# Two transformer blocks on one Trainium2 core: the eleven lanes of steps merged in another order

## The chip, the cores and the metric

The kernel runs on one core of one Trainium2 chip. Its time is the time of one execution on the device, in microseconds (us); lower is better. The profile shows one execution as the hardware profiler recorded it. Engines: PE is TensorE (matmuls), PEld its loads of weights, DVE VectorE, ACT ScalarE, POOL GpSimd, SP SyncE (it issues the loads from HBM).

## What is computed

Two blocks follow each other on 256 rows of width 1024, all in float32, each block with two layers. A layer of the first block runs a sparse attention and a gated delta rule side by side and mixes them:

```python
h = rms_norm(x, norm_gain[layer]);  proj = h @ w_in[layer]          # split into 12 parts
y_a = dsa_attention(q_a, k_a, v_a, q_i, k_i, w_i) * silu(z_a)       # attention over the top keys
qkv_b = silu(causal_depthwise_conv(qkv_b, conv_w[layer]))
o_b = chunked_gated_delta_rule(l2_normalize(q_b), l2_normalize(k_b), v_b, beta, g)
y_b = rms_norm(o_b, gdn_norm_gain[layer]) * silu(z_b)
x = x + (gates[0] * y_a + gates[1] * y_b) @ w_out[layer]
```

The result, normalised once more, is the memory `mem`; the second block starts from it with four branches per layer (latent attention, stick-breaking attention, forgetting attention, attention over the memory):

```python
h = x @ w_in                                   # split into 9 parts
mk, mv = split(mem @ w_mem_kv)
merged = sum(sigmoid(merge_r @ w_merge_up)[n] * ((y[n] * silu(gate_z[n])) @ w_branch[n]) for n in range(4))
x = layer_norm(alpha * x + merged @ w_out)
```

## The kernel before

**The products.** Each float32 operand is written as a higher and a lower part, and a product is three matmuls: high by high, high by low, low by high. The weights come in units: one unit is two rows of 128 by 512 of a weight matrix (the names in the code are a matrix and a place in it, as mkv.6, o1.2, h3.4, br21). For one unit SP loads `raw` (five buffers), ACT copies it to the higher part `w_hi` (L1347), POOL subtracts to get the lower part `w_lo` in two halves (L866, L868), and PE multiplies (`mm`, L907; matmuls in L926, L934, L941). `w_hi` and `w_lo` have three slots, so a split waits until PE has used the unit three before it. The order of the units is fixed by their lane.

**The other steps.** Between the units PE makes small products of the attentions and of the delta rule, and transposes (L962), in two halves of PSUM called `chain`, which steps take in turn: a step first waits until the step two before it has been emptied by ACT or DVE (`take`, L951). Steps that the text names: `hT`, `xT` transpose the normalised rows at the start of a layer; `norm_a`, `norm`, `norm_c` are the norm's steps on DVE and ACT (L1668 to L1674 are the four tiny operations of its square root, L1753 the scaling); `mix_b`, `mix`, `mT` mix the two paths (L2207, L2223) and transpose the result for w_out; `onorm` is the norm of the delta rule's output; `stat_1_0` its key's transposes after the convolution (`tap`, `conv`); `gT` transposes the merged branches of the second block; `lat_a`, `lat`, `lat_c` normalise its latents (L2256 is the scaling), `ckT` transposes them; `sbz` are the scores of the stick-breaking attention, emptied by L2269 and L2272; `ln_a`, `ln_s`, `ln` are the layer norm at the layer's end; `gmul` the gate's product on DVE; `drain` empties a bulk product; `gz`, `mu`, `br`, `o`, `h` are weight matrices.

**The order of the work.** `lanes()` (L299) writes the steps into eleven lanes, each with a fixed inner order: s splits, m bulk products, d and v their drains on ACT and DVE, c convolution, w gates, a and b chains, x mix, y merge, e layer norm. `ORDER` (L319) is a string with one letter per step, and `plan()` (L335) takes the next step of the lane that the letter names. Every engine then walks the one list and runs those steps for which it has a handler:

```python
def plan():
    steps = {lane: iter(x) for lane, x in lanes().items()}
    return [next(steps[lane]) for lane in ORDER]
...
            for step in PLAN:
                if step[2] in steps:
...
                    steps[step[2]](*step[3:])
```

Engines wait for each other by semaphores; the value that a wait wants is the step's place among those of its name in the list. So the order sets which step stands behind which on each engine, and nothing else.

Of the kernel before, what the change touches and what calls it, by code (L numbers as in the profile page):

```python
# [298 lines left out]
def lanes():  # L299
# [17 lines left out]


ORDER = (  # L319
    "aaaaasammssvamsmssaamaaasaacsccasscccssammcmmsmaacssmmaacssccsmmmamaaasasmdabsmaaabssmmcsmaammassdbm"  # L320
    "adbmssaaammsssammsbadamsabaamamsaaaamssacmasccmaamasbsbbmacccscmammssmsccsaacbcmmbssmambbsaaasssammb"
    "bdsaaaamsssdmmmmaassdwbbssmmmsamcbmmamssssbbdbbmmaaambabxxsasbmaabbbsddmxssbaamswwamaaamaassmamsdwaa"
    "mwbasxsxmmsdmsaxbmwxsaxxxbmbbmxaxvsvsssmssmmmammsmaammsdsaaammsssssvammmmaaaascasscmmsccasscmcassccm"
    "msmaammcmsacsmcasmsassdaaaammasassmmaambbsmambacmaaamdassmssbdbssmaamabammaaamssaaadmsscamacsmssssaa"
    "mmamccacccmssbbscbcmmcamssacammbbsssmabbsmaaamdssaaaammssdsammadmmaabbscbbbmaswmmssdsbbbaassmsssmaaw"
    "maabmmbambsbxmxxbmssdbbbmmsssdamawammaasaadswwmbamasxxbsamaamssbaxdbbwxsxxmmmxxxsssssvsmmsvasadmmmmm"
    "mmsaaaasassaassmmdsssssdssbsdsbbmmmmmmsmmmmammmmsssaassdaasmmbbsaadbbsmmmbsaaasmmbddabbmbbmssaaamvba"
    "bmbsssddmmbbadmmsssybbmbssbmaambdsymsbamdsyyavbymbysydvvmmyssdmvssvvvvdmsvvvdmmmmssdymmmmmmvvvssssss"
    "yvvsmmmmmmmvmmmvsseeessvvvvaeeessmmaaammmbmmmmmmssdmssssssssdmmmmmadsasmsbaaammmbbbaassdasssdbbmbmma"
    "asaamsbmbsddbmbbmaaabmsssvbbmbasmmsabbdmbddsssasmabbssmymmambayddssmbsmbdsssydvyysmsdbsyyvvmmydmmmmv"  # L330
    "svsmdvvvvmsvvyssssmmvvvmmyvvmvvmssemmmmmsseemmvvvveemmme"
)


# [2132 lines left out]
```

How the kernel before makes its waits and increments, by code:

```python
                def load(u):  # L802
                    name, w, k0, nk, _, _ = UNITS[p.sec][u]
                    old = raw_before(p, u)
                    if old:
                        sp.wait_ge(*o.after("gpsimd", old[0], old[1], "split", old[2]))
                    src = dview(w["src"], p.l)
                    if w["src"] == "w_branch":
                        k0 += 2 * int(w["lhs"][2])
# [15 lines left out]
                def load_memory(g, r):  # L825
                    if (p.l, g, r) == (0, 1, 0):
                        sp.wait_ge(*p.after("tensor", "vT", 1))
                        sp.dma_start(mem_raw, t["mem_2"].rearrange("a (r p) d -> p (a r) d", p=P)).then_inc(mem_in, 16)
# [1 line left out]
                def next_gain():  # L830
                    sp.wait_ge(*p.after("vector", "norm_c", 1))
                    if p.l == 0:
                        load_more()
                    load_gain(t["gains"][p.l + 1:p.l + 2, :])
# [1 line left out]
                def ln_rows():  # L836
                    sp.wait_ge(*o.after("vector", "mid", 0, "norm_c", 1))
                    if p.l:
                        sp.wait_ge(*o.after("vector", "two", p.l - 1, "ln", 1))
                    for i, dst in enumerate((gain, gain2)):
                        sp.dma_start(dst[:, :], t["ln_rows"][2 * p.l + i:2 * p.l + i + 1, :].broadcast_to([P, D])).then_inc(
                            ln_in, 16)
# [130 lines left out]
                def memT(r):  # L974
                    if r == 0:
                        pe.wait_ge(mem_in, 16)
                    c = take("memT", r)
```

## Time and profile before

| | us |
|---|---|
| median of three runs (lowest to highest) | 1060.01 (1059.55 to 1061.75) |
| span of the profiled execution | 1056.6 |
| PE busy | 1025.6 (97%) |
| POOL busy | 712.2 (67%) |
| DVE busy | 599.0 (57%) |
| ACT busy | 577.4 (55%) |

The profiled execution has its span alone, from the first instruction to the last; the runs were timed from outside and lie 3.4 us above it. Busy time says which engine carries the program; what can still be moved is read from the waits of that engine, and from what else ran beside the instruction that was waited for.

### The profile page before, as it was taken

How to read it: one execution, taken by the hardware profiler on the slowest of the kernel's cores; microseconds unless marked ns; L12 is line 12 of the kernel's file. 1: busy time of each engine (PE TensorE's matmuls, PEld its weight loads, DVE VectorE, ACT ScalarE, POOL GpSimd, SP SyncE). 2: the span in 40 equal slices, each digit the busy share in tenths (PEclk: the TensorE clock that was granted, in tenths of full speed). 3: DMA queues.
4: the chain of work that ended last, by engine and by line, in shares of the span. 5: the costliest groups of instructions: out<-in, count | busy, mean ns of one | idle time of the engine just before them, and what ended most of it. 6: DMA issues, size and time to landing. Idle time of an engine off the chain costs nothing.

```text
span 1056.6 us, 18561 instructions
## 1 busy us (share of the span) xinstructions
PE 1025.6 (97%) x7112; PEld 886.4 (84%) x7112; DVE 599.0 (57%) x1181; ACT 577.4 (55%) x968; POOL 712.2 (67%) x550
## 2 busy tenths in 40 slices
PE   8999999999999999999999998999999989999986
PEld 8988998888877988899888887788888768888875
DVE  4774366786565557246584563517446560646564
ACT  4754347656644574336656744445576534567652
POOL 4786537872648787556766645897366978744794
PEclk9999999999999999999999999999999999999999
DMA  8664434653425555435444332665233546423451
GB/s 294 192 179 122 139 101 131 173 156 107 134 100 153 180 165 157 140 84 157 141 139 141 115 125 87 209 191 158 81 113 120 186 140 216 133 91 108 140 183 57
DMA packets 80584, 151.59 MB, mean 143 GB/s; under 512 B 6448, under 2 KB 12400, under 8 KB 80496
## 3 DMA queue, kind: packets, MB, share of 16 engines
q1 hardware_dynamic: 80496, 150.41, 46.9%
q8 instruction: 57, 0.93, 0.4%
q14 instruction: 31, 0.25, 0.1%
HBM read 149.34 MB, written 1.05 MB: 142 GB/s over the span
## 4 chain that ended last, share of the span: by engine, by line
PE 88%; DVE 4%; ACT 3%; POOL 3%; issue 2%; DMA 0%; POOLq 0%; SPq 0%; DVEq 0%; ACTq 0%
PE bulk L941 53%; PE bulk L926 12%; PE chain L962 5%; PE chain L970 4%; PE chain L1039 4%; PE chain L1307 1%; PE bulk L934 1%; PE chain L1288 1%; ACT arena L1347 1%; PE chain L1163 1%; PE chain L1179 1%; POOL w_lo L868 1%; DVE arena L1846 1%; PE chain L1030 1%; POOL w_lo L866 1%
## 5 line engine op out<-in xcount | busy, mean ns | idle before, releaser
L866 POOL TENSOR_TENSOR w_lo<-raw,w_hi 128x512 fp32r<-128x512 f32 (+3 forms) x259 | 340.7, 1316 | 292.4 <-ACT w_hi L1347 291.8
L868 POOL TENSOR_TENSOR w_lo<-raw,w_hi 128x512 fp32r<-128x512 f32 (+3 forms) x277 | 375.6, 1357 | 31.8 <-ACT w_hi L1347 31.8
L1347 ACT ACTIVATE w_hi<-raw 128x1024 fp32r<-128x1024 f32 (+4 forms) x277 | 277.3, 1019 | 210.1 <-PE bulk L941 163.4
L941 PE MATMUL bulk<-w_hi,hT_hi 128*128 128x512 f32 (+1 forms) x756 | 306.0, 405 | 0.8 <-ACT arena L1347 0.5
L941 PE MATMUL bulk<-w_hi,hT_lo 128*128 128x512 f32 (+1 forms) x756 | 294.4, 389 | 0.0
L941 PE MATMUL bulk<-w_lo,hT_hi 128*128 128x512 f32 (+1 forms) x756 | 204.2, 389 | 1.9 <-POOL w_lo L868 1.9
L941 PEld LDWEIGHTS bulk<-w_hi,hT_hi 128*128 128x128 f32 x756 | 142.4, 188 | 33.5 <-issue 1.9
L941 PEld LDWEIGHTS bulk<-w_lo,hT_hi 128*128 128x128 f32 x756 | 141.7, 188 | 32.7 <-POOL w_lo L868 3.4
L941 PEld LDWEIGHTS bulk<-w_hi,hT_lo 128*128 128x128 f32 x756 | 142.5, 188 | 26.8 <-issue 1.0
L926 PE MATMUL bulk<-hT_hi,w_hi 128*128 128x256 f32 x384 | 96.3, 289 | 0.0
L926 PE MATMUL bulk<-hT_lo,w_hi 128*128 128x256 f32 x384 | 94.0, 282 | 0.0
L962 PE MATMUL chain<-cst,arena 128*128 128x128 f32 (+1 forms) x544 | 73.4, 276 | 7.8 <-DVE arena L2223 3.5
L962 PEld LDWEIGHTS chain<-cst,arena 128*128 128x128 f32 (+1 forms) x544 | 62.7, 142 | 15.1 <-issue 9.3
L926 PEld LDWEIGHTS bulk<-hT_hi,w_hi 128*128 128x128 f32 x384 | 73.4, 191 | 0.9 <-ACT w_hi L1347 0.7
L1347 ACT ACTIVATE arena<-chain 128x512 f32<-128x512 f32 (+4 forms) x64 | 45.5, 727 | 52.0 <-PE chain L962 23.6
L926 PEld LDWEIGHTS bulk<-hT_lo,w_hi 128*128 128x128 f32 x384 | 73.5, 191 | 0.0
L1846 DVE SCALAR_TENSOR_TENSOR arena<-bulk,par,arena 128x253 f32<-128x253 f32 (+2 forms) x144 | 59.4, 475 | 21.0 <-ACT arena L1347 19.0
L1342 ACT ACT_TABLE_LOAD x44 | 56.5, 1283 | 26.5 <-PE bulk L941 14.3
L1347 ACT ACTIVATE arena<-bulk 128x1024 f32<-128x1024 f32 (+2 forms) x50 | 50.1, 1006 | 17.3 <-PE bulk L941 17.2
L926 PE MATMUL bulk<-hT_hi,w_lo 128*128 128x256 f32 x384 | 53.9, 283 | 0.0
L1347 ACT ACTIVATE arena<-arena,tiny 128x256 f32<-128x256 f32 (+1 forms) x80 | 36.2, 454 | 27.0 <-DVE tiny L2345 19.4
L926 PEld LDWEIGHTS bulk<-hT_hi,w_lo 128*128 128x128 f32 x384 | 49.5, 192 | 0.0
(262 smaller groups left out, 1393.4 us busy)
## 6 DMA issues: line engine op xcount, KB each, us to landing
raw<-in_w_in_dram SPq DMA_DIRECT2D x194, 512.0 KB, 3.6
raw<-in_w_out_dram SPq DMA_DIRECT2D x32, 512.0 KB, 3.7
raw<-in_w_branch_dram SPq DMA_DIRECT2D x16, 512.0 KB, 3.7
raw<-in_w_mem_kv_dram SPq DMA_DIRECT2D x8, 512.0 KB, 3.4
raw<-in_w_merge_up_dram SPq DMA_DIRECT2D x16, 256.0 KB, 2.9
raw<-in_w_in_dram SPq DMA_DIRECT2D x8, 420.0 KB, 3.4
gain<-in_ln_rows_dram SPq DMA_DIRECT2D x4, 512.0 KB, 5.3
gain<-in_gains_dram SPq DMA_DIRECT2D x3, 512.0 KB, 6.1
```

What stands on the lines that cost most here:

```text
L866: pool.tensor_tensor(lo_of(p, u)[:, 0:at], raw_of(p, u)[:, 0:at], hi_of(p, u)[:, 0:at].bitcast(F32), ALU.subtract).then_inc(first_part, 1)
L868: pool.tensor_tensor(lo_of(p, u)[:, at:n], raw_of(p, u)[:, at:n], hi_of(p, u)[:, at:n].bitcast(F32), ALU.subtract).then_inc(p.done("split" ...
L926: m = pe.matmul(dst, part[:, k, j * P:(j + 1) * P], b[:, kk, :], start=(not low and kk == 0 and i == 0 and j % 2 == 0), stop=(low and kk = ...
L934: m = pe.matmul(pair[0:n, 0:S], part[:, k, :], b[:, kk, :], start=(not low and kk == 0 and i == 0), stop=(low and kk == tot - 1))
L941: m = pe.matmul(dst, a, part[:, k, :], start=(first and not low and k == 0 and i == 0), stop=(last and low and k == nk - 1))
L962: m = pe.transpose(c[0:n, i * P:i * P + v.shape[0]], v, ident[0:v.shape[0], 0:v.shape[0]])
L970: m = pe.matmul(c[at, col + j * HALF:col + (j + 1) * HALF], a, b, start=(j == 0), stop=(j == R * 4 - 1), skip_group_check=True)
L1030: pe.matmul(c[:, j * P:(j + 1) * P], spread(4 * r + j, 8), rows_T[0:8, :], start=(j == 0), stop=(j == 3), skip_group_check=True)
L1039: m = pe.matmul(c[:, j * P:(j + 1) * P], a, b, start=(j == 0), stop=(j == 3), skip_group_check=True)
L1342: act.preload_act_table_set(sets[func])
L1347: return act.activation(dst, src, func, **more)
L1846: ins = STT(cv[:, j, back:S], b[:, j * S:(j + 1) * S - back], par1[:, p.l, c:c + 1], cv[:, j, back:S], ALU.mult, ALU.add)
```

## The change

`ORDER` is another string, of the same letters, each as often as before. Nothing else differs: lanes, handlers, buffers and waits are the same code. Of its twelve lines one:

```diff
 ORDER = (
-    "aaaaasammssvamsmssaamaaasaacsccasscccssammcmmsmaacssmmaacssccsmmmamaaasasmdabsmaaabssmmcsmaammassdbm"
+    "aaaaasavssmmaamsamsmasasasaacmmmccscsmacccassaamsmcmsssmaacmcmscmamassadssabammsaaacammmasmsmmbmdssa"
...
```

At the change of layer in the first block, on ACT, from the last splits of layer 0 on (`hT_hi<-chain` empties the transposes hT, `w_hi<-raw` are splits, the last three wide ones before hT being mkv.2, mkv.4 and mkv.6, `mkv<-bulk` empties that product). Before:

```order
L1347 ACTIVATE w_hi<-raw 128x1024 [waits mm_tensor,raw_in2]
L1347 ACTIVATE arena,tiny<-xs 128x1024 [waits drain_v_vector,x_loaded]
L1347 ACTIVATE w_hi<-raw 128x1024 [waits mm_tensor,raw_in3]
L1347 ACTIVATE tiny<-tiny 128x2 [waits norm_a_vector]
L1347 ACTIVATE tiny<-tiny 128x2 [waits scalar_step]
L1347 ACTIVATE w_hi<-raw 128x1024 [waits mm_tensor,raw_in4]
L1347 ACTIVATE mkv<-bulk 128x1024 [waits mm_tensor]
L1347 ACTIVATE w_hi<-raw 128x704 [waits mm_tensor,raw_in0]
L1347 ACTIVATE hT_hi<-chain 128x1024 [waits rows_turned_tensor] x2
```

And now:

```order
L1347 ACTIVATE w_hi<-raw 128x1024 [waits mm_tensor,raw_in2]
L1347 ACTIVATE w_hi<-raw 128x1024 [waits mm_tensor,raw_in3]
L1347 ACTIVATE arena,tiny<-xs 128x1024 [waits drain_v_vector,x_loaded]
L1347 ACTIVATE tiny<-tiny 128x2 [waits norm_a_vector]
L1347 ACTIVATE tiny<-tiny 128x2 [waits scalar_step]
L1347 ACTIVATE hT_hi<-chain 128x1024 [waits rows_turned_tensor]
L1347 ACTIVATE w_hi<-raw 128x1024 [waits mm_tensor,raw_in4]
L1347 ACTIVATE hT_hi<-chain 128x1024 [waits rows_turned_tensor]
L1347 ACTIVATE w_hi<-raw 128x704 [waits mm_tensor,raw_in0]
L1347 ACTIVATE w_hi<-raw 128x1024 [waits mm_tensor,raw_in1]
L1347 ACTIVATE mkv<-bulk 128x1024 [waits mm_tensor]
```

The split of mkv.6 (raw_in4) and the emptying of its product have moved behind the emptying of the transposes.

At the end of layer 1 of the first block, on ACT, from the emptying of the last gate product on (`gain<-bulk`; `arena,tiny<-arena` are the sums of squares of `onorm_a`, the table load and the tiny operations are `onorm`, raw_in1 is unit o1.2, the last row empties mT_1). Before:

```order
L1347 ACTIVATE hT_hi<-chain 128x1024 [waits rows_turned_tensor,mm_tensor]
L1347 ACTIVATE gain<-bulk 128x1024 [waits gmul_vector,mm_tensor]
L1347 ACTIVATE arena,tiny<-arena 128x128 [waits o_vector]
L1347 ACTIVATE arena,tiny<-arena 128x128 [waits scalar_step] x7
L1347 ACTIVATE w_hi<-raw 128x1024 [waits mm_tensor,raw_in1]
L1342 ACT_TABLE_LOAD [waits onorm_a_vector]
L1347 ACTIVATE tiny<-tiny 128x2x4
L1347 ACTIVATE tiny<-tiny 128x2x4 [waits scalar_step]
```

And now:

```order
L1347 ACTIVATE gain<-bulk 128x1024 [waits gmul_vector,mm_tensor]
L1347 ACTIVATE hT_hi<-chain 128x1024 [waits rows_turned_tensor,mm_tensor]
L1347 ACTIVATE arena,tiny<-arena 128x128 [waits o_vector]
L1347 ACTIVATE arena,tiny<-arena 128x128 [waits scalar_step] x7
L1342 ACT_TABLE_LOAD [waits onorm_a_vector]
L1347 ACTIVATE tiny<-tiny 128x2x4
L1347 ACTIVATE tiny<-tiny 128x2x4 [waits scalar_step]
L1347 ACTIVATE w_hi<-raw 128x1024 [waits mm_tensor,raw_in1]
```

The gate product is emptied ahead of the transposes mT_0, and the split of o1.2 has moved behind the table load and the norm's two operations.

In layer 1 of the second block, on DVE, at the latents (L1668 to L2256 are `lat_c`, the pairs L2269 and L2272 empty `sbz`). Before:

```order
L2269 SCALAR_TENSOR_TENSOR arena<-chain,cst 128x1024
L2272 SCALAR_TENSOR_TENSOR arena<-arena 128x1024
L2269 SCALAR_TENSOR_TENSOR arena<-chain,cst 128x512
L2272 SCALAR_TENSOR_TENSOR arena<-arena 128x512
L1668 TENSOR_TENSOR tiny<-tiny 128x4
L1670 TENSOR_TENSOR tiny<-tiny 128x4
L1672 TENSOR_SCALAR tiny<-tiny 128x4
L1674 TENSOR_TENSOR tiny<-tiny 128x4
L2256 SCALAR_TENSOR_TENSOR arena<-arena,tiny,par 128x384 x2
L2256 SCALAR_TENSOR_TENSOR arena<-arena,tiny,par 128x256 x2
```

And now:

```order
L1668 TENSOR_TENSOR tiny<-tiny 128x4
L1670 TENSOR_TENSOR tiny<-tiny 128x4
L1672 TENSOR_SCALAR tiny<-tiny 128x4
L1674 TENSOR_TENSOR tiny<-tiny 128x4
L2256 SCALAR_TENSOR_TENSOR arena<-arena,tiny,par 128x384 x2
L2256 SCALAR_TENSOR_TENSOR arena<-arena,tiny,par 128x256 x2
L2269 SCALAR_TENSOR_TENSOR arena<-chain,cst 128x1024
L2272 SCALAR_TENSOR_TENSOR arena<-arena 128x1024
L2269 SCALAR_TENSOR_TENSOR arena<-chain,cst 128x512
L2272 SCALAR_TENSOR_TENSOR arena<-arena 128x512
```

`lat_c` has moved ahead of the emptying of both `sbz`.

## Rows read from the trace of the kernel before

**Rows 1.** The page, busy time of the engines, and the chain by engine.

```profile
PE 1025.6 (97%) x7112; PEld 886.4 (84%) x7112; DVE 599.0 (57%) x1181; ACT 577.4 (55%) x968; POOL 712.2 (67%) x550
...
PE 88%; DVE 4%; ACT 3%; POOL 3%; issue 2%; DMA 0%; POOLq 0%; SPq 0%; DVEq 0%; ACTq 0%
```

**Rows 2.** What PE waited for, whole span; us in total, times, longest us.

```profile
PE chain L962 <- DVE arena L2223: 3.5, 2, 2.9
...
PE chain L962 <- DVE arena L1828: 2.7, 1, 2.7
...
PE bulk L934 <- DVE hT_lo L1759: 1.4, 1, 1.4
```

**Rows 3.** PE's timeline; start, us, engine, line, operation, tiles, count, [idle before <-releaser].

```profile
635.47 0.39 PE L941 MATMUL bulk<-w_hi,hT_hi 128*128 128x512 f32 x1
...
638.19 0.39 PE L941 MATMUL bulk<-w_hi,hT_hi 128*128 128x512 f32 x1
...
643.92 1.94 PE L962 MATMUL chain<-cst,arena 128*128 128x128 f32 x8 [2.85 <-DVE arena L2223]
...
645.51 0.78 PE L941 MATMUL bulk<-w_hi,hT_hi 128*128 128x512 f32 x1
...
649.08 0.39 PE L941 MATMUL bulk<-w_hi,hT_hi 128*128 128x512 f32 x1
```

**Rows 4.** DVE's timeline, layer norm at the change of layer in block one.

```profile
334.38 1.21 DVE L1670 TENSOR_TENSOR tiny<-tiny 128x2 f32<-128x2 f32 x1
...
335.62 1.22 DVE L1672 TENSOR_SCALAR tiny<-tiny 128x2 f32<-128x2 f32 x1
...
336.88 1.20 DVE L1674 TENSOR_TENSOR tiny<-tiny 128x2 f32<-128x2 f32 x1
```

**Rows 5.** POOL's timeline, the same stretch.

```profile
334.29 1.28 POOL L868 TENSOR_TENSOR w_lo<-raw,w_hi 128x512 fp32r<-128x512 f32 x1
...
336.78 1.28 POOL L868 TENSOR_TENSOR w_lo<-raw,w_hi 128x512 fp32r<-128x512 f32 x1
```

**Rows 6.** POOL's and DVE's timeline, the layer norm ahead of block two.

```profile
668.81 1.29 POOL L868 TENSOR_TENSOR w_lo<-raw,w_hi 128x512 fp32r<-128x512 f32 x1
...
670.16 0.16 DVE L1674 TENSOR_TENSOR tiny<-tiny 128x2 f32<-128x2 f32 x1
```

**Rows 7.** ACT's timeline, the end of layer 1 of block one.

```profile
635.73 1.06 ACT L1347 ACTIVATE w_hi<-raw 128x1024 fp32r<-128x1024 f32 x1 [0.96 <-PE bulk L941]
...
636.81 1.28 ACT L1342 ACT_TABLE_LOAD   x1
```

**Rows 8.** PE's timeline, two single waits, at stat_1_0 and at gz1.0.

```profile
380.81 1.06 PE L962 MATMUL chain<-cst,arena 128*128 128x128 f32 x8 [0.69 <-ACT arena L1347]
...
773.36 0.50 PE L941 MATMUL bulk<-w_hi,hT_hi 128*128 128x512 f32 x1 [0.53 <-ACT arena L1347]
```

**Rows 9.** DVE's timeline, the mix at the ends of layers 0 and 1.

```profile
288.52 2.19 DVE L2223 TENSOR_TENSOR arena<-arena 128x1024 f32<-128x1024 f32 x1
...
640.23 2.19 DVE L2207 SCALAR_TENSOR_TENSOR arena<-arena,tiny 128x128 f32<-128x128 f32 x8
...
642.55 1.22 DVE L2223 TENSOR_TENSOR arena<-arena 128x1024 f32<-128x1024 f32 x1
```

**Rows 10.** DVE's timeline, L2256 in layers 0 and 1 of block two.

```profile
715.19 4.86 DVE L2256 SCALAR_TENSOR_TENSOR arena<-arena,tiny,par 128x384 f32<-128x384 f32 x4
...
911.32 1.94 DVE L2256 SCALAR_TENSOR_TENSOR arena<-arena,tiny,par 128x384 f32<-128x384 f32 x4
```

**Rows 11.** Stretches: busy us of PE, PEld, DVE, ACT, POOL; PEclk, DMA share, GB/s.

```profile
645.00:646.00 1.00, 1.00 (x6) 0.99 (x5) 0.00 (x0) 0.05 (x1) 0.00 (x0) 0.50 0.00 0
```

**Rows 12.** ACT's timeline, change of layer in block two.

```profile
863.71 1.99 ACT L1347 ACTIVATE w_hi<-raw 128x1024 fp32r<-128x1024 f32 x2
```

**Rows 13.** DVE's timeline, eviction of sbz_0 in layer 1 of block two.

```profile
907.41 1.69 DVE L2272 SCALAR_TENSOR_TENSOR arena<-arena 128x1024 f32<-128x1024 f32 x1
```

**Rows 14.** POOL's timeline, start of its last unbroken run.

```profile
1010.39 1.37 POOL L866 TENSOR_TENSOR w_lo<-raw,w_hi 128x512 fp32r<-128x512 f32 x1 [0.86 <-ACT w_hi L1347]
```

More of the change, by code:

```diff
@@ L319 @@
 ORDER = (
-    "aaaaasammssvamsmssaamaaasaacsccasscccssammcmmsmaacssmmaacssccsmmmamaaasasmdabsmaaabssmmcsmaammassdbm"
[L321 to L329, printed above, removed]
@@ L330 @@
-    "asaamsbmbsddbmbbmaaabmsssvbbmbasmmsabbdmbddsssasmabbssmymmambayddssmbsmbdsssydvyysmsdbsyyvvmmydmmmmv"
-    "svsmdvvvvmsvvyssssmmvvvmmyvvmvvmssemmmmmsseemmvvvveemmme"
+    "aaaaasavssmmaamsamsmasasasaacmmmccscsmacccassaamsmcmsssmaacmcmscmamassadssabammsaaacammmasmsmmbmdssa"
+    "dsabbsambssamsaaasmamaabsadamamasaamsasaccsmamcasamabbscsmamcccbmsacssscmmascbsmcmammdssmabasbbsmsbb"
+    "ambmdamaasbssmbamsdasamsbsmmaawsbmcssmmdabmabasammsbabmxsmxasbawbsambasddbssaabsmamwaaaambamwaxmmsss"
+    "admswsaxaxdsmmaxbwxsmaxxxbmbbxamxmmsmmsvvsmmssssaammaaasasmsvdmmmsaassmmsasmacscamcssamsccmssamccacm"
@@ new lines @@
+    "mssaacmmcsssmcammadbsmsabmassaaaasmcsamsmaammambsabadasambabsaamadbaamsmaamsaasmasasmasmmaadccscssma"
+    "sbcasmccmcbsasmscmmsaamsmmccbbmsasbcsaammabaxscasmsmadbaasbmmdbmsmmsasbbbsmwdassbsmmssmmmasbbmxmbaba"
+    "dsbamsxsdabasbbsaasmabamsdasswssmwmbammwmdmaawsaamabsxamaasxmasbawdxbbmxmxmxsxxxsssmvsvasmmmsmmsmama"
+    "aasasssasmamdmmmmsmssmsdmssamsmsbsdsdsbmsmmbmamsssasammabmmsassaddmabasabbbmamaddmabbasasbbmsbavmmbm"
+    "sbsbsmdsdmybmbasmsbbsmdbssbmbamsmyadbamydysvsbmaysbyydvmmsvysmdvmssvmvmvdmsvmsdssyvmdssvsvsmmmvssvvy"
@@ L332 @@
+    "vvvmssveesmemmvmmmvmvmsmmvemaesemasmaammsmsbmamsmsmsmmmsdmsmmsssdmdambsmmssbssaamabdaamamsmdsmsbbbsb"
+    "asaamsmbbddbsmabbmmbasabbamssadbmbvmbbssmasdsamsabbmmabyssmmyddabsydsbmssdsysmvymdbysyvsdvmmymvvvmms"
+    "svdmsmmsvmmdsvvvsysvmmvssvyvvmmmvmmvsessmememvvvmvemeemm"
 )
```

## Prediction

> **What bounds the kernel now.** I read the page's busy line and its chain first, then TensorE's (PE's) waits, then the stretches in which those waits lie. PE is busy 1025.6 of 1056.6 us, and the chain that ended last is PE for 88% [rows 1]. So the work itself stays, and another order of the same steps can win or lose only what PE idles, some 31 us with the start and the end. The waits [rows 2] show where: 3.5 us in two before the transposes mT of the mixed rows, at the end of a layer of block one (2.9 us of it in one); 2.7 us before the transposes gT near the program's end; then a microsecond or two behind the Vector engine (DVE) at each change of layer, like the 1.4 us before the narrow product L934. A steady unit of the bulk product is 12 matmuls, from 635.47 to 638.19 us: 2.72 us [rows 3].
>
> The second thing to see is that DVE and GpSimd (POOL) hold each other up. The tiny operations L1670 to L1674 of the layer norm take about 1.2 us each from 334.38 us on [rows 4], and each ends within 0.1 us of the end of one of POOL's subtractions [rows 5]. At 670.16 us the same L1674 takes 0.16 us, just after POOL's last subtraction has ended at 670.10 [rows 6]. Which split of a weight unit falls beside which chain on DVE is set by the order, and that is where this change acts.
>
> **The change, part by part.** No arithmetic is added. The Activation engine (ACT) loads its function table 47 times instead of 44, at 1.28 us [rows 7]. I cost the three at nothing, because the splits behind them are ready some units ahead; without that cover each could cost PE its 1.28 us. The stream of weight units, its slots and its loads on SP are the same. The loads of the layer norm's rows move, in each layer of block two, past a few weight loads on SP; these rows are wanted only at the layer's end, so I cost that at nothing too; if a weight load came late by it, PE would wait for that one load.
>
> First place, the change of layer in block one (333 to 382 us). Unit mkv.6, its split and its product, goes from before the transposes hT to behind hT_0 and hT_1. POOL then is idle from 335.57 us, and two of the tiny operations drop from 1.2 to about 0.17 us: hT starts 2.1 us sooner. But mkv.6 now waits behind hT_0: eviction and split on ACT (about 1.06 us each, as the split of [rows 7]), then two subtractions of 1.28 us on POOL [rows 5]; it ends 0.9 us after its own 2.72 us would. The 1.4 us for which PE waited for hT's eviction is covered by it. Laid end to end from mkv.4's end, the narrow product ends 0.3 us sooner. The wait of 0.69 us before the transposes stat_1_0, at 380.81 us [rows 8], goes too, since the last tap of the convolution now stands on DVE ahead of the statistics. Together -1.0 us.
>
> Second place, the end of layer 1 (628 to 661 us). On DVE the gate product goes ahead of mT_0's lower part, so o0.0 starts 0.6 us later. On ACT the split of o1.2 goes behind the output norm's table load and activations [rows 7], which then start 0.9 us sooner, and L2207 on DVE starts at about 638.6 instead of 640.23 us. If nothing else happened, mT_1 would start at 642.4 instead of 643.92 us, and PE would have idled 0.8 us instead of 3.0, too little for the clock to fall. The unit behind mT_1, at half clock, runs from 645.51 to 649.08 us, 3.57 us instead of 2.72 [rows 3]. That is -1.5 and -0.9, in sum -2.4 us. But the two subtractions of o1.2's split now fall into L2207's eight operations, which before ran beside an idle POOL in 2.19 us [rows 9]. No row shows L2207 beside a busy POOL. The nearest is L2256, again one operation on two tensors in SBUF: four of them took 4.86 us beside a busy POOL and 1.94 us beside an idle one [rows 10]. So the delay lies between 0 and two subtractions (2.6 us) in L2207, and 0 to 1 us in L2223, which took 2.19 us once and 1.22 us here [rows 9]. I take the end that L2256 gives for L2207, 2.5 us, and none for L2223: mT_1 at 644.7 us, +0.8. PE then idles 3.1 us, and the granted clock falls to half (1.2 GHz) behind it as it did before (0.50 at 645 us, [rows 11]), so nothing is won there. The Trainium skill's page "SBUF — State Buffer", section "Who interferes with whom", says that a DVE instruction with two inputs in SBUF contends with a GpSimd instruction that reads SBUF, and that the later one blocks for the whole instruction. By that rule this place costs +0.8 us; without it, it would give -2.4. No run yet shows it for L2207.
>
> Third, the layer norm behind that (660 to 676 us). mkv.6 moves between the first transposes xT as it did above. The tiny operations lose 2.1 us of waiting, and the late split gives nearly all of it back: -0.3 us.
>
> Block two, layer 0: the wait of 0.53 us at 773.36 us [rows 8] goes, because the evictions of gz0 and mu2 stand further ahead on ACT, and some tenths behind it: -0.8 us. Moving gT_1 ahead of two bulk units makes PE wait some 3 us for the merge, but POOL's splits set the pace of that stretch up to o1.6, so I cost it at nothing; if PE were the pace there, it would cost those 3 us.
>
> Change of layer in block two (853 to 877 us): the layer norm's first step for the second half of the rows goes ahead of xT's lower part on DVE. ACT's activations for it, and the two splits queued behind them at 863.71 us [rows 12], start 1.1 us sooner, and so do POOL and the product h1.4: -1.1 us.
>
> Layer 1, the latents (900 to 916 us): lat_c goes ahead of sbz's evictions on DVE, and between the products sbz and the transposes ckT_0 stands one bulk unit instead of three. Its 2.72 us must cover the eviction of sbz_0, of which L2272 alone takes 1.69 us [rows 13], and which starts only after lat_c: +0.8 us.
>
> The end: ACT splits br21 before it empties mu7, so POOL's unbroken run from 1010.39 us, ahead of which it idled 0.86 us [rows 14], starts sooner; br31's slot, freed by PE, limits that: -0.4 us.
>
> The other moves lie in stretches where PE hardly waited. Steps of one chain placed back to back can wait a few tenths for an eviction, and others lose such a wait; I put these at 0, with -3 and +4 us as the bounds. The sum is -1.0 + 0.8 - 0.3 - 0.8 - 1.1 + 0.8 - 0.4 = -2.0 us against the profiled span of 1056.6. The median of the runs, 1060.0, lies 3.4 us above that span; I take this to stay: 1058.0 us. A difference under 0.2%, 2.1 us, can't be told from none.
>
> **The rivals.** (a) POOL does not hold L2207. For it: L2207 took 2.19 us wherever it is seen. Against it: L2256. The second place then gives -2.4 instead of +0.8: 1054.8 us.
>
> (b) Slower: the latents of layer 1. lat_c's four tiny operations and its four L2256 now come before sbz's eviction. If POOL is busy through them, eight operations of about 1.2 us take the place of four of 0.16 and 1.94 us [rows 6, 10], 7 us more; they start some 2 us sooner, since the step before them has fewer splits beside it. So sbz's eviction and ckT_0 come about 5 us late, with one unit of cover where there were three: 1058.0 + 5.0 = 1063.0 us. It decides whether POOL begins the split of h3.4 before lat's activations on ACT are through. The order on ACT has that split behind them, which speaks against; for it speaks that POOL was busy beside L2256 in layer 0 [rows 10].
>
> (c) Nothing: with PE at 97%, waits only change places: 1060.0 us. For it speaks that most of PE's waits are ends of chains that every order has.
>
> **How the numbers follow.** My sum has 0.45, half of it beyond 0.2% and half within, as 1058.0 lies on that line: 0.22 faster, 0.23 the same. (a) has 0.22, all faster; (b) 0.18, all slower; (c) 0.15, of which 0.10 the same, 0.04 slower, 0.01 faster. So faster 0.45, same 0.33, slower 0.22. The range reaches to (b), takes in (a), and beyond it the nearer part of the bound of -3: 1053.0 to 1063.0 us. The likeliest case alone has 1056 to 1060 us.
>
> **What would show it.** L1672 and L1674 at 0.17 us at the change of layer in block one; L2207 at 4 us or more with POOL busy beside it, mT_1's wait still near 3 us with half clock behind it; no wait before gz1.0; ckT_0 waiting about 1 us or less. The forecast is wrong if L2207 stays at 2.19 us, if lat_c takes over 6 us, or if PE shows waits of over 1 us in stretches that were full before.

## The result and the profile after

| | kernel before | changed kernel |
|---|---|---|
| median (lowest to highest), us | 1060.88 (1059.55 to 1062.17), 4 runs | 1072.98 (1071.20 to 1076.64), 4 runs |
| ratio, 95% interval | | 1.012 [1.0092, 1.0147] |
| span of the profiled execution, us | 1056.6 | 1074.8 |

The changed order is slower by 1.2%, outside the forecast's range. In every execution whose span and time are both known, the span lies 1.7 to 2.0 us below its own time (1076.64 and 1074.8 here). So the profiled execution of the kernel before took about 1058.4 us (an estimate from its span), 2.5 us less than the median beside it, and that of the changed kernel was its slowest of four, 3.7 us over its median. Of the 18.1 us between the two traces some 6 us belong to the two executions and 12 to the change. One run of a later kernel (the changed one with short subtractions, 1119.35 us) lay over 1.5% above the fastest of its kernel and is left out of median and ratio.

The page's row of busy times, changed kernel (compare [rows 1]):

```profile
PE 1032.0 (96%) x7112; PEld 891.3 (83%) x7112; DVE 633.9 (59%) x1181; ACT 580.6 (54%) x971; POOL 716.4 (67%) x550
```

DVE is 34.9 us busier than before with the same 1181 instructions on the same data. An instruction that is held counts as busy, so this is, in the main, time in which DVE's instructions were held. What PE waited for, changed kernel (total us, times, longest; compare [rows 2]):

```profile
PE chain L970 <- DVE arena L1973: 4.6, 2, 4.4
PE chain L962 <- DVE arena L2368: 4.4, 1, 4.4
PE chain L962 <- DVE arena L1828: 4.4, 2, 2.5
PE chain L962 <- DVE arena L1753: 3.5, 3, 2.0
PE chain L962 <- DVE arena L2223: 3.2, 2, 2.5
```

The first two are new. Where they lie is seen by setting the end of the same PE step in the two traces side by side (ends of the last matmul, from PE's timelines):

| PE step | before, us | changed, us | behind by |
|---|---|---|---|
| block one, layer 0, unit 42 | 174.53 | 174.83 | 0.30 |
| unit 64, after x1_1 and sc_0 | 263.18 | 271.11 | 7.93 |
| mkv.4, ahead of hT | 336.74 | 344.67 | 7.93 |
| layer 1, unit 11 | 380.13 | 389.93 | 9.80 |
| stat_1_0 | 381.89 | 390.81 | 8.92 |
| unit 71 and what belongs to it, o_1_0 | 622.24 | 632.73 | 10.49 |
| unit 77, behind mT_1 | 651.98 | 663.14 | 11.16 |
| block two, layer 0, unit 30 | 776.39 | 787.51 | 11.12 |
| unit 32, after qk2T_0 | 786.27 | 803.58 | 17.31 |
| last unit of layer 0 | 859.27 | 876.75 | 17.48 |
| layer 1, unit 0, second half | 876.96 | 893.51 | 16.55 |
| unit 22 | 935.19 | 951.66 | 16.48 |
| last unit | 1048.33 | 1066.47 | 18.14 |

Two steps hold 13.8 us: 7.6 around x1_1 (a product of the delta rule's blocks, in layer 0) and 6.2 at qk2T_0 (transposes of queries and keys in block two). In neither place did PE wait before.

**x1_1.** It waits for L1973, eight small products on DVE. DVE's and POOL's timelines, changed kernel:

```profile
218.63 9.09 DVE L1973 TENSOR_TENSOR arena<-tiny,cst 128x64 f32<-128x64 f32 x8
...
217.68 1.29 POOL L866 TENSOR_TENSOR w_lo<-raw,w_hi 128x512 fp32r<-128x512 f32 x1
218.94 1.29 POOL L868 TENSOR_TENSOR w_lo<-raw,w_hi 128x512 fp32r<-128x512 f32 x1
...
226.38 1.26 POOL L868 TENSOR_TENSOR w_lo<-raw,w_hi 128x512 fp32r<-128x512 f32 x1
...
227.87 1.97 PE L970 MATMUL chain<-cst,arena 64*64 64x64 f32 x32 [4.38 <-DVE arena L1973]
```

Kernel before, the same step:

```profile
209.06 3.47 DVE L1973 TENSOR_TENSOR arena<-tiny,cst 128x64 f32<-128x64 f32 x8
...
209.79 1.40 POOL L866 TENSOR_TENSOR w_lo<-raw,w_hi 128x512 fp32r<-128x512 f32 x1 [0.51 <-ACT w_hi L1347]
```

Before, POOL paused 0.51 us: the first six of the eight got through there in 0.2 to 0.3 us each, the last two were held for 1.3 us each, and the eight took 3.47 us. Now POOL subtracts without a break until 227.6 us. The first of the eight waits for the rest of the running subtraction, each of the others for a whole one: 9.09 us. On ACT the emptying of a gate product now stands ahead of two splits, which then come together at 211.06 us, and POOL works off what has gathered. PE idles 4.38 us, and the matmuls behind run at the lower of its two levels (1.2 GHz; granted 0.50 from 227 to 231 us).

**qk2T_0.** It waits for rope_2 (L2104 to L2368, small operations on DVE). Changed kernel, DVE and POOL:

```profile
782.67 1.01 DVE L2104 TENSOR_TENSOR arena<-arena,cos_t 128x128 f32<-128x128 f32 x1
783.60 1.35 DVE L2104 TENSOR_TENSOR arena<-arena,sin_t 128x128 f32<-128x128 f32 x1
...
786.46 1.32 DVE L2107 TENSOR_TENSOR arena<-arena 128x32 f32<-128x32 f32 x1
787.70 1.29 DVE L2108 TENSOR_TENSOR arena<-arena 128x32 f32<-128x32 f32 x1
789.03 1.42 DVE L2367 COPY arena<-arena 128x512 f32<-128x512 f32 x1
790.37 1.35 DVE L2368 COPY arena<-arena 128x256 f32<-128x256 f32 x1
...
786.44 1.29 POOL L866 TENSOR_TENSOR w_lo<-raw,w_hi 128x512 fp32r<-128x512 f32 x1 [1.63 <-ACT w_hi L1347]
```

Kernel before:

```profile
773.33 0.19 DVE L2107 TENSOR_TENSOR arena<-arena 128x32 f32<-128x32 f32 x1
773.44 0.18 DVE L2108 TENSOR_TENSOR arena<-arena 128x32 f32<-128x32 f32 x1
773.66 0.43 DVE L2367 COPY arena<-arena 128x512 f32<-128x512 f32 x1
774.00 0.29 DVE L2368 COPY arena<-arena 128x256 f32<-128x256 f32 x1
```

Allowing for the 11.3 us by which the changed kernel is behind, rope_2 starts at the same moment in both (782.67 and 771.34 us). Its first two operations are held by an earlier pair of subtractions (1.01 and 1.35 us instead of 0.29 and 0.28), which makes the last four 1.8 us later. These then take 5.4 us instead of 1.1, because POOL's next run begins at 786.44 us, 0.02 us ahead of them; before, it began behind them. COPY, with one operand in SBUF, is held like the others. The Trainium skill's page "SBUF — State Buffer", section "Who interferes with whom", counts copies among the operations that can contend, and here the trace agrees: 1.42 us instead of 0.43.

**The places the prediction named.** In block one at the change of layer, and at mT_1:

```profile
337.99 5.62 DVE L1738 CUSTOM_DVE_ANT_0 arena<-xs 128x1024 f32<-128x1024 f32 x1 [0.17 <-DVE xs L1779]
...
344.73 0.17 DVE L1672 TENSOR_SCALAR tiny<-tiny 128x2 f32<-128x2 f32 x1
344.93 0.16 DVE L1674 TENSOR_TENSOR tiny<-tiny 128x2 f32<-128x2 f32 x1
...
649.44 4.04 DVE L2207 SCALAR_TENSOR_TENSOR arena<-arena,tiny 128x128 f32<-128x128 f32 x8 [0.49 <-DVE tiny L2071]
...
654.98 1.44 PE L962 MATMUL chain<-cst,arena 128*128 128x128 f32 x8 [2.53 <-DVE arena L2223]
```

L1672 and L1674 take 0.17 us, as forecast. In this execution L1670 does too, since L1738 (the sum of squares ahead of them, 1.86 us in the trace of before) was held until POOL's run was over. Where L1738 was held for one subtraction only (the run with both places put back, below), L1670 took 1.21 us and L1672 0.17 us, just as the prediction has it. L2207 is held by two subtractions, as forecast.

### The profile page after: what moved, and what is told of

It reads as the page before. It is cut to its first block and busy times, and to the rows that moved or that the text cites. A ratio compares the mean times of both kernels' runs of the same rounds, so it can differ in the third digit from the quotient of the medians.

```text
span 1074.8 us, 18569 instructions
## 1 busy us (share of the span) xinstructions
PE 1032.0 (96%) x7112; PEld 891.3 (83%) x7112; DVE 633.9 (59%) x1181; ACT 580.6 (54%) x971; POOL 716.4 (67%) x550
## 5 line engine op out<-in xcount | busy, mean ns | idle before, releaser
L962 PE MATMUL chain<-cst,arena 128*128 128x128 f32 (+2 forms) x544 | 75.5, 281 | 16.4 <-DVE arena L2368 4.4
L962 PEld LDWEIGHTS chain<-cst,arena 128*128 128x128 f32 (+2 forms) x544 | 63.4, 143 | 25.6 <-issue 17.6
L1347 ACT ACTIVATE arena<-arena 128x128 f32<-128x128 f32 (+2 forms) x65 | 37.8, 584 | 14.0 <-DVE arena L1924 9.7
```

Of the source, the lines that this page charges most:

```text
L962: m = pe.transpose(c[0:n, i * P:i * P + v.shape[0]], v, ident[0:v.shape[0], 0:v.shape[0]])
L1347: return act.activation(dst, src, func, **more)
```

## The experiments

The theory (H): a DVE operation of the kinds seen in [rows 4] and [rows 10] is held while one of POOL's subtractions runs, so a chain of small DVE operations costs one subtraction per operation when POOL works without a break; the change moved POOL's runs beside two such chains. Its main rival (C): the new order leaves those steps too little cover on PE, and the hold is by the way. Ratios are to the kernel before, run on the same chip. The changed kernel was not run again beside these kernels, so a gain over it is the difference of two ratios, and by their intervals uncertain by some 4 us either way; what a single edit does is therefore read from the traces first.

**One operation instead of eight.**

```diff
-for r in range(R):
-    for j in range(4):
-        ins = TT(xth[:, 4 * r + j, :].rearrange("p (b i) -> p b i", i=BLK),
-                 over(inv[:, 4 * r + j, :], HALF // BLK), blocks, ALU.mult)
+shape = [P, R * 4, HALF // BLK, BLK]
+TT(xth[:, :, :].rearrange("p m (b i) -> p m b i", i=BLK), inv[:, :, :].unsqueeze(2).broadcast_to(shape),
+   blocks.unsqueeze(1).broadcast_to(shape), ALU.mult)
...
```

> The changed kernel, with the eight operations of L1973 (128 x 64 each) written as one of 128 x 512: the same products, order and waits. Theory H (hold): each DVE operation with two SBUF operands waits for one of POOL's subtractions, whatever its length, so in the changed kernel L1973 took 9.09 us beside an unbroken POOL. One operation waits once: L1973 at about 2 us or less, x1_1 of layer 0 without its 5.3 us of waiting, the time 4 to 5.5 us lower, 1068. Rival C (cover): the order puts x1_1 too near to its sources, and the hold is by the way; then only the eight starts go, about 1 us, and the time stays at 1072.

Measured: 1069.67 us, ratio 1.0083 [1.0057, 1.0110]. DVE's timeline:

```profile
218.64 0.87 DVE L1972 TENSOR_TENSOR arena<-tiny,cst 128x512 f32<-128x512 f32 x1
219.55 2.19 DVE L1838 TENSOR_TENSOR arena<-arena,gain 128x1024 f32<-128x1024 f32 x1
```

The operation starts where L1973 started (218.64 against 218.63 us) and takes 0.87 us; PE's wait for it is gone from its list of waits, and unit 64 ends 1.8 us behind the trace of before instead of 7.9. H holds, C falls at this place. From 1.0120 to 1.0083 is 3.9 us, a little under the 4 to 5.5 expected. (The 5.3 us of waiting here and in the expectation for rope_2 stand in no view; the profile's idle time is 4.4 us at both.)

> The kernel before, with L1973 as one operation in the same way. There L1973 took 3.47 us and PE did not wait for it. H and C both expect no difference: 1060.0 to 1060.9 us. If it is faster by over 2 us, waits on DVE that PE doesn't show count in some other way, and both are wrong.

Measured: the same edit in the kernel before gives 1062.08 us, 1.0003 [0.9976, 1.0031]: no difference, as both expected.

**One letter at rope_2.** The letter `d` (mu3) moves ahead of three splits:

```diff
-    "sbsbsmdsdmybmbasmsbbsmdbssbmbamsmyadbamydysvsbmaysbyydvmmsvysmdvmssvmvmvdmsvmsdssyvmdssvsvsmmmvssvvy"
+    "sbsbsmdsdmybmbadsmsbbsmbssbmbamsmyadbamydysvsbmaysbyydvmmsvysmdvmssvmvmvdmsvmsdssyvmdssvsvsmmmvssvvy"
```

> The changed kernel with one letter moved: ACT empties mu3 ahead of the splits of gz1's next two units, not behind the third. On DVE, POOL, PE and SP nothing moves. H: POOL's run of subtractions starts 1 us later, at about 787.4 instead of 786.4 us, when most of rope_2 on DVE is over; L2107 to L2368 take 1.2 to 2.5 us together instead of 5.4, the wait before qk2T_0 falls from 5.3 to 1 us or less, the time by 4 to 5 us, to about 1068.5. C: rope_2 stands behind the same steps and PE has the same units as cover, so nothing changes: 1073.

Measured: 1067.90 us, 1.0066 [1.0039, 1.0093], by the ratios 5.7 us below the changed kernel. DVE's and POOL's timelines:

```profile
781.98 0.19 DVE L2107 TENSOR_TENSOR arena<-arena 128x32 f32<-128x32 f32 x1
782.31 0.43 DVE L2367 COPY arena<-arena 128x512 f32<-128x512 f32 x1
...
782.87 1.28 POOL L866 TENSOR_TENSOR w_lo<-raw,w_hi 128x512 fp32r<-128x512 f32 x1 [2.54 <-ACT w_hi L1347]
```

The run on POOL starts 0.89 us after L2107 instead of 0.02 us ahead of it; the four operations take 0.2 to 0.4 us each and PE waits for none of them. One operation on ACT, about 1 us long, decided over 5 us on PE. C, by which nothing would change, falls here too.

**Both places back.** In slices of the two strings:

```diff
-ORDER = changed
+ORDER = changed[:175] + before[175:251] + changed[251:754] + before[754:849] + changed[849:]
```

> The changed kernel, with the order of the kernel before in two stretches: from the last units of layer 0's convolution to x1 and sc (the 76 letters from place 175), and in block two, layer 0, around rope_2 (95 letters from place 754). If these two places hold the loss (7.8 and 6.4 us between the two traces), the time is 1058.5 to 1061, the kernel before within 1.5 us. If the loss is spread (a rival: every denser stretch costs a little), 1065 or more remains.

Measured: 1065.45 us, 1.0033 [1.0016, 1.0051]. By the times about 9 of the 12 us are gone; 3.5 us over the kernel before remain, where at most 1.5 were expected. But that does not show a loss spread over the rest: in this trace PE has two waits inside the first stretch put back, which neither kernel has there:

```profile
240.47 1.50 PE L962 MATMUL chain<-cst,arena 128*128 128x128 f32 x12 [1.87 <-ACT arena L1347]
...
242.92 1.13 PE L1179 MATMUL chain<-arena 128*128 128x128 f32 x8 [0.95 <-ACT arena L1347]
```

Old and new order joined there make waits of their own: PE falls 3.0 us behind between the units that end at 223.4 and 263.2 us in the trace of before. How much is spread over the other stretches this run leaves open. In this execution L1738 took 1.89 us, not 5.62.

**A longer subtraction.** POOL's two subtractions of a unit become one:

```diff
-pool.tensor_tensor(lo_of(p, u)[:, 0:at], raw_of(p, u)[:, 0:at],
-                   hi_of(p, u)[:, 0:at].bitcast(F32), ALU.subtract).then_inc(first_part, 1)
-pool.tensor_tensor(lo_of(p, u)[:, at:n], raw_of(p, u)[:, at:n],
-                   hi_of(p, u)[:, at:n].bitcast(F32), ALU.subtract).then_inc(p.done("split"), 1)
+pool.tensor_tensor(lo_of(p, u)[:, 0:n], raw_of(p, u)[:, 0:n],
+                   hi_of(p, u)[:, 0:n].bitcast(F32), ALU.subtract).then_inc(p.done("split"), 1)
...
```

> The changed kernel, with POOL's two subtractions of a unit (128 x 512 each) made one of 128 x 1024; PE waits for it ahead of the first lower matmul, at most 1.3 us earlier than it needs. H, told more exactly: a DVE operation with two SBUF operands gets in when POOL's running subtraction ends, and the next subtraction follows behind it; so the hold lasts one POOL instruction. With instructions of about 2.5 us the eight of L1973 beside an unbroken POOL take 16 to 20 us instead of 9.1, tiny operations up to 2.4 us instead of 1.2, and the time rises to 1085 or more. Rival S (the two share the path, both slowed by the bytes that they move): the bytes are the same, L1973 stays at 8 to 10 us, the time at 1073 to 1078.

Measured: 1100.42 us, 1.0378 [1.0336, 1.0420], though POOL is busy 48.8 us less (667.6 us). rope_2 on DVE, and POOL (lines are 7 lower in this kernel):

```profile
796.48 2.38 DVE L2100 TENSOR_TENSOR arena<-arena 128x32 f32<-128x32 f32 x1
798.99 2.45 DVE L2360 COPY arena<-arena 128x512 f32<-128x512 f32 x1
...
796.44 4.72 POOL L863 TENSOR_TENSOR w_lo<-raw,w_hi 128x1024 fp32r<-128x1024 f32 x2 [1.81 <-ACT w_hi L1340]
```

The hold lasts as long as the subtraction: 2.4 us instead of 1.3. Rival S falls. The edit also lets PE wait for a whole unit's subtraction; only 1.9 us of PE's waits are for that, so most of the loss lies elsewhere, but it was not split up further. L1973 itself was not hit: POOL happened to pause and the eight took 3.22 us, so the 16 to 20 us were not seen.

**A split behind a wait on ACT.** In the changed kernel, ACT, POOL and PE at unit 65 of layer 1:

```profile
595.08 1.28 ACT L1342 ACT_TABLE_LOAD   x1 [12.74 <-PE chain L1163]
...
598.49 1.29 POOL L866 TENSOR_TENSOR w_lo<-raw,w_hi 128x512 fp32r<-128x512 f32 x1 [11.70 <-ACT w_hi L1347]
...
605.74 0.50 PE L941 MATMUL bulk<-w_lo,hT_hi 128*128 128x512 f32 x1 [0.73 <-POOL w_lo L868]
```

```diff
-    "dsbamsxsdabasbbsaasmabamsdasswssmwmbammwmdmaawsaamabsxamaasxmasbawdxbbmxmxmxsxxxsssmvsvasmmmsmmsmama"
+    "dsbamsxsabasbbsaadsmabamsdasswssmwmbammwmdmaawsaamabsxamaasxmasbawdxbbmxmxmxsxxxsssmvsvasmmmsmmsmama"
```

> The changed kernel with one letter moved: in layer 1 of block one ACT empties zb0 behind the next two splits instead of ahead of them. In the changed kernel that step waits 12.7 us for the scores sc_1_1, the splits stand behind it, POOL idles 11.7 us, and unit 65 comes 1.0 us late. If the queue behind that wait is the cause, unit 65 waits for nothing and the time is 1 us lower, 1072. Rival: the splits done early put POOL beside the delta rule's operations on DVE, and as much is lost there: 1073 or more.

Measured: 1070.94 us, 1.0100 [1.0070, 1.0131]; unit 65 no longer waits. The place is shown; the gain of about 1 us is too small for the interval.

**The three edits together.**

> The changed kernel with the edits of three runs at once: L1973 as one operation, mu3 emptied ahead of the splits, zb0 behind them. If the losses add, 3.5 + 5 + 1 us go: 1063 to 1064, and against the kernel before 1.000 to 1.003. If each mended place only hands its wait to the next, 1067 or more.

Measured: 1065.08 us, 1.0045 [1.0027, 1.0063]. All three waits are gone from PE's list. From 1.0120 to 1.0045 is 8.0 us, where 9.5 were expected and the three edits alone add up to 11.7: the losses add in the main, within the intervals, and 4.8 us over the kernel before remain, more than expected. In its trace they lie in many places of about 1 us or less (PE waits 1.2 us ahead of the transposes yT_3 and 0.8 us at the decay step dec_1_0, for instance). Which of them repeat was not tried one by one.

**What the changed order does better.** In slices: `before[:387] + changed[387:403] + before[403:930] + changed[930:936] + before[936:]`, and L1973 as one.

> The kernel before, with the changed order in two short stretches where the traces show it ahead: around the convolution's last tap and stat_1_0 of layer 1 (16 letters from place 387, 0.88 us) and at the layer norm's second half in block two (6 letters from place 930, 0.9 us), and L1973 as one operation. My sum: 1.8 us below the kernel before, ratio 0.9983. Rival: waits only change places, ratio 1.000; or POOL comes to stand beside another DVE chain, 1.002 or more.

Measured: 1059.46 us, 0.9999 [0.9979, 1.0018]. In the trace the wait at stat_1_0 is gone, but PE still waits 0.9 us, as before, for the layer norm's last step on DVE at block two's change of layer: the second stretch alone gives nothing. The interval holds both the sum's 0.9983 and the rival's 1.000: no gain can be told.

**Fewer operations on the layer norm's chain**, in the kernel before, with the stretch at stat_1_0 and the one operation for L1973 of the run above:

```diff
-TT(tmp, y, y, ALU.mult)
-TT(tmp, tmp, x, ALU.mult)
-TS(tmp, tmp, -0.5, 1.5, ALU.mult, ALU.add)
-TT(y, y, tmp, ALU.mult)
+TT(tmp, y, x, ALU.mult)
+STT(tmp, tmp, -0.5, y, ALU.mult, ALU.mult)
+STT(y, tmp, 1.5, y, ALU.add, ALU.mult)
```

> The kernel before with three edits: the stretch around stat_1_0 in the changed order (16 letters from place 387), L1973 as one operation, and the square root's four tiny operations L1668 to L1674 written as three (two of them with two multiplications in one; its rounding differs in the last bit). H: beside POOL the number of operations costs, not their length. At the layer norm of both changes of layer in block one the four took about 1.2 us each on the chain to hT and to xT, so one less gives about 1.2 us at each, and stat_1_0 0.9 us: 3.3 us, ratio 0.997. Rival: PE's wait there is set by something behind (the split of w_lo, hT's own emptying) and the sum is 0.9 us at most, ratio 0.999 to 1.000.

Measured: 1062.13 us, 1.0002 [0.9979, 1.0025]: a miss, near the rival. DVE's timeline (L1736 and L1751 are L1738 and L1753 of the other kernels):

```profile
334.02 3.13 DVE L1736 CUSTOM_DVE_ANT_0 arena<-xs 128x1024 f32<-128x1024 f32 x1 [0.17 <-DVE xs L1777]
...
339.79 0.16 DVE L1672 SCALAR_TENSOR_TENSOR tiny<-tiny 128x2 f32<-128x2 f32 x1
339.99 4.89 DVE L1751 SCALAR_TENSOR_TENSOR arena<-xs,tiny,gain 128x512 f32<-128x512 f32 x4
```

The tiny operations save 3.3 us, but the sum of squares ahead of them is held 1.3 us longer than in the trace of before, and the scaling behind them is held too: 4.89 us instead of 2.86. From the start of the one to the end of the other the chain takes 10.9 us in both traces. At this place fewer operations only moved the hold to their neighbours.

**One more unit ahead of mT_1.** In ORDER the `m` of unit 76 moves ahead of the `x` of mT_1:

> The kernel of the run before this one, and in layer 1 of block one unit 76 goes ahead of the transposes mT_1 on PE, four units ahead of them instead of three. PE waits 3.9 us for mT_1 in the kernel before; 2.7 us of it go, but the unit behind mT_1 needs its lower part, about 2.3 us after it (ACT 1.0, DVE 1.2). Net 0.4 us lower, and up to 0.7 more if neither wait is long enough for the clock to fall: ratio 0.996. Rival: the two waits together are as long and the clock falls behind both: ratio 0.998.

Measured: 1061.44 us, 0.9997 [0.9977, 1.0017]. The wait ahead of mT_1 (2.85 us in the profile [rows 3]; the expectation's 3.9 stands in no view) is replaced by one for its lower part, and the unit behind runs at half clock (0.50 granted at 649 us):

```profile
647.87 0.50 PE L941 MATMUL bulk<-w_hi,hT_hi 128*128 128x512 f32 x1 [2.50 <-DVE hT_lo L2224]
```

The rival had the mechanism right: nothing won.

**Shorter subtractions.** Each of POOL's subtractions cut into two of 128 x 256:

```diff
+for a, b in ((0, at), (at, n)):
+    for lo, up in ((a, (a + b) // 2), ((a + b) // 2, b)):
...
+            ins = pool.tensor_tensor(lo_of(p, u)[:, lo:up], raw_of(p, u)[:, lo:up],
+                                     hi_of(p, u)[:, lo:up].bitcast(F32), ALU.subtract)
...
```

> The kernel before, with each of POOL's subtractions (128 x 512) cut into two of 128 x 256. From the runs: 1.28 us for 512 columns, 2.39 us for 1024, so 0.17 us of each is fixed and 256 columns take about 0.73 us (estimate), a unit 2.9 us on POOL, over PE's 2.72. H: DVE operations beside POOL wait 0.7 us instead of 1.25; the chains to hT and xT get 2 to 4 us shorter, and in long rows of bulk units POOL becomes the pace by 0.2 us a unit. Net between -3 and +6 us; I take 1062. Rival S (shared path): holds as long as before, POOL the pace: 1068 or more.

> The changed kernel, with POOL's subtractions cut into two in the same way. H: what the changed order loses to holds shrinks with the length of a subtraction: L1973 takes 5 to 6 us instead of 9.1, L2107 to L2368 about 3 instead of 5.4, so the changed order stands 4 to 8 us behind the kernel of the run before this one instead of 12. Rival C (the order itself): the distance stays at 11 to 13 us.

Measured: kernel before 1101.36 us, 1.0392 [1.0357, 1.0426]; changed kernel 1102.73 us, 1.0365 [1.0302, 1.0428]. From the changed kernel with the short subtractions, POOL's busy row on the page and DVE at L1973 (here L1976):

```profile
L867 POOL TENSOR_TENSOR w_lo<-raw,w_hi 128x256 fp32r<-128x256 f32 (+3 forms) x1072 | 782.5, 769 | 283.4 <-ACT w_hi L1350 283.0
...
219.53 5.49 DVE L1976 TENSOR_TENSOR arena<-tiny,cst 128x64 f32<-128x64 f32 x8
```

L1973 falls to 5.49 us, as H said, rope_2's last four operations to 2.5 us, and the changed order no longer stands behind the other: by the ratios the distance of 12 us is -3 us, uncertain by some 8. That speaks against C, but not strictly, since POOL's pace now covers much of what the order does. Both are 40 us slower; my estimate of 1062 was far off. A subtraction of 256 columns takes 0.77 us, a unit 3.1 us against PE's 2.72, and POOL becomes the pace of long rows of units (14 waits of PE for w_lo, 9.9 us, in the kernel before with short subtractions). Long holds, told below, add to it: behind the longest PE waits 14.3 us. The rest of the 40 us was not traced.

## Why the prediction was wrong

**The step that failed** is "The other moves lie in stretches where PE hardly waited ... I put these at 0, with -3 and +4 us as the bounds". I searched the waits that exist and asked which the new order removes. The new waits arose where none was: x1_1 (+7.6 us between the traces, behind 9.09 us of held L1973) and qk2T_0 (+6.2, behind rope_2's 5.4 us), against a bound of +4 for all such places together. The forecast had the mechanism, from [rows 4 to 6] and [rows 10], and applied it to L2207 and L2256 alone. The trace of before had L1973 in its short version (3.47 us where eight of 0.21 us each would do); a list of all DVE chains on which PE's steps depend, with what POOL does beside them in the new order, would have shown both.

**The gain that caused a loss.** "the wait of 0.53 us at 773.36 us [rows 8] goes", because drains stand further ahead on ACT. It fell to 0.28 us in the trace. But with the emptying of mu3 moved behind three splits, these came earlier too, POOL's run met rope_2, and PE paid over 5 us: the one-letter run shows that.

**Point by point**, forecast and trace (differences of the table's kind):

- Change of layer in block one: -1.0 forecast, +1.0 in this execution (+1.9 at the narrow product, -0.9 at stat_1_0, the latter as forecast). L1738's 5.6 us took most of what the tiny operations gave: from its start to the end of the scaling 10.0 us instead of 10.9. Where L1738 was held once only (both places back) this chain took 8.9 us, 2.0 less, as forecast, and yet the stretch gives only +0.2 and -0.9: -0.6. The narrow product did not come sooner.
- End of layer 1: +0.8 forecast, +0.7 in the trace (10.49 to 11.16). L2207 took 4.04 us where I took 4.7; PE waited 2.53 us ahead of mT_1 where I had 3.1; the unit behind started at half clock. The step held, and rival (a) is out.
- The layer norm ahead of block two: -0.3 forecast, +0.2.
- gT_1 in block two, layer 0, costed at nothing: +2.1 at the transposes, and 0.6 ahead of them and 1.7 behind them given back. The step held.
- Change of layer in block two: -1.1 forecast, -0.9. But it is not worth that by itself: the run with this stretch alone kept the wait.
- Latents of layer 1: +0.8 forecast, 0.0. Rival (b) had half its mechanism: L2256 took 5.05 us for four instead of 1.94 [rows 10], though the tiny operations took 0.16 us; ckT_0 still found its input in time.
- The end: -0.4 forecast, 0.0.
- Among the others: unit 65 in layer 1, about +1.1, and some 1.6 us in small steps in layer 1 of block two.
- "The median of the runs, 1060.0, lies 3.4 us above that span; I take this to stay": every execution with both numbers shows 1.7 to 2.0. The profiled one was a quick one, and I took its distance for a constant.

## What to carry to other kernels

When an order changes, the waits of the old trace tell what can be won, not what can be lost: list every chain of small operations that feeds the critical engine, and ask what runs beside each in the new order. On an engine that shares a path, an edit that makes work earlier can cost more than one that makes it late; here an operation of 1 us on ACT, moved by a letter, decided 5 us. Fewer operations on the held side helped where eight became one (a wait of 4.4 us went), and did not where four became three: there the neighbours were held instead.

## What the runs showed of the hardware

Not every DVE operation is held. Beside the run that held L1973, L1965 and L1968, each with one operand in PSUM (`chain`), took 0.17 to 0.22 us from 215.43 us on.

A held operation usually gets in when the running subtraction ends, but not always. L1738 (128 x 1024) stands ahead of the layer norm in block one beside a run of POOL in every kernel here. With subtractions of 512 columns it took 1.82 to 1.89 us in seven profiled executions (one subtraction waited for), 3.13 and 3.14 us in the two kernels with three tiny operations, 5.62 and 5.65 us in the changed kernel and the one with one operation for L1973; with subtractions of 256 columns 7.15 us in both. In the changed kernel and in the one with both places put back it starts 0.49 us into a subtraction, with three more to come in both; in the first it waits for all of them, in the second for the running one alone, and POOL's next one is held instead (2.28 us). What decides this is not shown. With the short subtractions one addition waited through 24 of them and got in only when POOL stopped:

```profile
853.87 17.10 DVE L1831 TENSOR_TENSOR arena<-arena 128x1024 f32<-128x1024 f32 x1
...
853.40 11.04 POOL L867 TENSOR_TENSOR w_lo<-raw,w_hi 128x256 fp32r<-128x256 f32 x16
864.39 2.78 POOL L867 TENSOR_TENSOR hT_lo<-raw,hT_hi 128x256 fp32r<-128x256 f32 x4
867.11 2.78 POOL L867 TENSOR_TENSOR sT_lo<-raw,sT_hi 128x256 fp32r<-128x256 f32 x4
```

The Trainium skill's page "SBUF — State Buffer", section "Who interferes with whom", says that the later of the two blocks for the whole instruction. Where a waiting operation gets in at the first boundary the trace agrees (1.3 us each beside subtractions of 1.29 us at rope_2). L1831 does not fit: it had waited since 853.87 us, 23 of the 24 subtractions began later, and it went last.

Who wins a turn also differs from one execution to the next. In the kernel before, with L1973 as one operation, L2187 (L2189 elsewhere) fell on the start of a subtraction and was held, and an addition behind it met the next run; the order is the same there:

```profile
261.31 1.32 DVE L2187 TENSOR_SCALAR tiny<-tiny 128x4 f32<-128x4 f32 x1
...
266.06 3.34 DVE L2077 TENSOR_TENSOR arena<-arena,par 128x512 f32<-128x512 f32 x2
```

In the trace of before:

```profile
260.81 0.17 DVE L2189 TENSOR_SCALAR tiny<-tiny 128x4 f32<-128x4 f32 x1
...
264.42 1.29 DVE L2079 TENSOR_TENSOR arena<-arena,par 128x512 f32<-128x512 f32 x2
```

PE waited 2.1 us for it at invZ_1_3 (L1095), where it waited for nothing in the other trace. The kernels with three tiny operations, without and with the unit moved, are the same program up to this place. The operation starts 0.01 us ahead of a subtraction in both; in the first it is held, in the second not:

```profile
261.00 1.32 DVE L2185 TENSOR_SCALAR tiny<-tiny 128x4 f32<-128x4 f32 x1
...
260.33 0.17 DVE L2185 TENSOR_SCALAR tiny<-tiny 128x4 f32<-128x4 f32 x1
```

The 24 runs of the kernel before beside the first four experiments span 1057.25 to 1068.20 us. That such chances make up this whole spread is argued from these traces, not shown.
